# Redistributing the modulation matrix's chunks over the stages of a two-block kernel

## The reference

```python
cs = jax.nn.silu(c)
for layer in range(DEPTH):
    mod = jnp.matmul(cs, ada_w[layer]) + ada_b[layer]
    sh_m, sc_m, g_m, sh_f, sc_f, g_f = [m[:, None, :] for m in jnp.split(mod, 6, axis=-1)]
    h = modulate(x, norm_mix_g[layer], sh_m, sc_m)
    y = (even_mixer, odd_mixer)[layer](h, ...)
    x = x + (g_m * y).astype(x.dtype)
    h = modulate(x, norm_ffn_g[layer], sh_f, sc_f)
    x = x + (g_f * conv_glu_ffn(h, ...)).astype(x.dtype)
```

## Time and profile before

| | |
|---|---|
| time, median of 3 runs | 2181.15 us (2172.75 to 2181.36) |
| the profiled execution's own time | 2180.79 us |
| its span, first to last instruction | 2179.0 us |
| mean granted clock of TensorE | 0.976 |
| TensorE busy | 95% |
| VectorE, ScalarE, GpSimd busy | 48%, 36%, 36% |
| read from HBM | 199.1 MB, 92 GB/s over the span |

### The profile page before, as it was taken

One profiled execution on the slowest core, in us unless ns is written; L12 is line 12 of the kernel. 1 busy time (PEld: TensorE's weight loads), 2 busy tenths in 40 slices (PEclk: granted clock), 3 DMA queues, 4 the chain that ended last, 5 costly groups with the idle time before them and its releaser, 6 DMA issues.

```text
span 2179.0 us, 22946 instructions
## 1 busy us (share of the span) xinstructions
PE 2062.0 (95%) x9468; PEld 1572.6 (72%) x9468; DVE 1053.4 (48%) x1507; ACT 780.9 (36%) x1186; POOL 782.9 (36%) x333
## 2 busy tenths in 40 slices
PE   7998999889999999997999998999999999999998
PEld 5765667588856679884778877886975577788886
DVE  6356575654466666914275546635601343211233
ACT  3332564423355332135342312324355433322231
POOL 3313363134354344221234334433423233434432
PEclk9999999999989999998999999999999999999999
DMA  5226202155510244110125344423311022233321
GB/s 177 90 89 161 78 1 68 60 175 173 174 59 21 97 135 136 59 59 20 58 77 160 111 134 137 149 90 97 97 59 39 20 97 78 78 97 98 108 62 62
DMA packets 202728, 203.54 MB, mean 93 GB/s; under 512 B 11871, under 2 KB 199523, under 8 KB 202624
## 3 DMA queue, kind: packets, MB, share of 16 engines
q1 hardware_dynamic: 200953, 200.90, 28.9%
q0 software_dynamic: 656, 1.01, 0.3%
q10 hardware_dynamic: 1015, 0.16, 0.0%
HBM read 199.10 MB, written 2.10 MB: 92 GB/s over the span
## 4 chain that ended last, share of the span: by engine, by line
PE 69%; DVE 14%; ACT 7%; POOL 6%; DMA 2%; issue 2%; SPq 0%; DVEq 0%; ACTq 0%; POOLq 0%
PE bank L505 40%; PE bank L950 14%; POOL wl L2024 6%; ACT wh L1164 3%; PE bank L687 2%; DVE var L1578 2%; DVE acc L1546 2%; PE bank L711 1%; PE bank L807 1%; PE bank L736 1%; DVE conv L1917 1%; DVE conv L1919 1%; PE bank L1009 1%; DVE conv L1915 1%; PE bank L1030 1%
## 5 line engine op out<-in xcount | busy, mean ns | idle before, releaser
L2024 POOL TENSOR_TENSOR wl<-ring,wh 128x2048 fp32r<-128x2048 f32 (+3 forms) x150 | 643.0, 4288 | 1099.3 <-ACT wh L1164 1099.3
L1164 ACT ACTIVATE wh<-ring 128x2048 fp32r<-128x2048 f32 (+3 forms) x150 | 265.1, 1768 | 286.1 <-PE bank L950 95.3
L1546 DVE SCALAR_TENSOR_TENSOR acc<-ring,cs,acc 128x256 f32<-128x256 f32 x336 | 287.5, 856 | 12.0
L505 PE MATMUL bank<-xfh,wh 128*128 128x512 f32 x704 | 278.2, 395 | 15.6 <-POOL wl L2024 12.7
L505 PE MATMUL bank<-xfh,wl 128*128 128x512 f32 x704 | 275.0, 391 | 0.0
L505 PE MATMUL bank<-xfl,wh 128*128 128x512 f32 x704 | 274.9, 391 | 0.0
L505 PEld LDWEIGHTS bank<-xfh,wh 128*128 128x128 f32 x704 | 132.6, 188 | 51.1 <-POOL wl L2024 17.4
L505 PEld LDWEIGHTS bank<-xfh,wl 128*128 128x128 f32 x704 | 132.6, 188 | 28.2
L1894 DVE SCALAR_TENSOR_TENSOR x<-bank,mod,x 128x512 f32<-128x512 f32 x48 | 34.7, 750 | 243.0 <-PE bank L950 243.0
L505 PEld LDWEIGHTS bank<-xfl,wh 128*128 128x128 f32 x704 | 132.8, 189 | 26.6
L950 PE MATMUL bank<-hsph,wh 128*128 128x512 f32 x352 | 138.8, 394 | 4.7 <-POOL wl L2024 4.7
(11 more groups left out here) (386 smaller groups left out, 4277.4 us busy)
## 6 DMA issues: line engine op xcount, KB each, us to landing
ring<-in_ada_w SPq DMA_DIRECT2D x48, 1024.0 KB, 5.3
ring<-in_ffn_w_in SPq DMA_DIRECT2D x44, 1024.0 KB, 5.2
ring<-in_w_in_b SPq DMA_DIRECT2D x14, 1024.0 KB, 5.3
ring<-in_even_w_in SPq DMA_DIRECT2D x14, 1024.0 KB, 5.2
ring<-in_ffn_w_out SPq DMA_DIRECT2D x16, 768.0 KB, 4.9
ring<-in_odd_w_in SPq DMA_DIRECT2D x12, 1024.0 KB, 5.3
ring<-in_ffn_w_out SPq DMA_DIRECT2D x16, 640.0 KB, 4.4
ring<-in_w_out SPq DMA_DIRECT2D x8, 1024.0 KB, 5.1
```

Source lines behind the costliest of these rows:

```text
L505: mm = eng.matmul(o, l_, r_, start=(first and i == 0), stop=(last and i == 2))
L1164: eng.activation(wh[:, m % SPLIT, 0:w], ring[:, n % RING, 0:w], ACT.Copy).then_inc(wh_ready, 1)
L1546: ins = eng.scalar_tensor_tensor(out=s, in0=w[:, k, :], scalar=cs[:, k:k + 1], in1=s, op0=ALU.mult, op1=ALU.add)
L2024: eng.tensor_tensor(wl[:, m % SPLIT, 0:w], ring[:, n % RING, 0:w], wh[:, m % SPLIT, 0:w].bitcast(F32), ALU.subtract).then_inc(wl_ready, 1)
```

## The change

The ada chunks stand elsewhere in the plan, by explicit lists: none in the first gate projection; none behind the first chunk of layer b's value projection and one behind each of the 13 others; none behind the even mixer's first chunk (5 there); in the first FFN's third and fifth pair of part one a second one, between a and g; seven in the odd mixer, behind the last three qk chunks and the four v chunks. VectorE's calls follow: `ada_steps(6)` before the rotations goes, 15 becomes 13, 6 becomes 5, two steps instead of one in the two FFN pairs, and in the odd mixer one step behind the convolutions of tiles 3, 5 and 7 and four behind the last. The modulation is taken in four parts of 24 columns, when 19, 24, 41 and 48 sums are made (`ADA_UNTIL`): before the even mixer, behind the even mixer's ada steps, in the FFN's second part, and in the odd mixer before `gcol`. `shift` on ScalarE waits for its own part. TensorE has an `ada_sums(0)` more behind the even mixer's ia chunks and one behind v, and `lag=1` in qk and v of the odd mixer.

```diff
-ADA_FIRST = 26
+ADA_UNTIL = (19, 24, 41, 48)
+ADA_TWICE = {0: (2, 4), 12: ()}
...
-    def add(chunks, per=0):
+    def add(chunks, behind=()):
         for n, c in enumerate(chunks):
             plan.append(c)
-            for _ in range((n + 1) * per // len(chunks) - n * per // len(chunks)):
+            for _ in range(behind[n] if n < len(behind) else 0):
                 plan.append(ada.pop(0))
...
-    add(k8("in_a.gate", w, 928, 1952), 6)
+    add(k8("in_a.gate", w, 928, 1952))
...
-    add(k8("out_a", a["w_out"][0], 0, D), 3)
+    add(k8("out_a", a["w_out"][0], 0, D), (0, 1, 1, 1))
...
-        + k8("in_b.k", w, MAIN, 2 * MAIN), 15)
-    add(k8("out_b", a["w_out"][1], 0, D), 3)
+        + k8("in_b.k", w, MAIN, 2 * MAIN), (0,) + 13 * (1,))
+    add(k8("out_b", a["w_out"][1], 0, D), (0, 1, 1, 1))
...
+    for name, lo, behind in (("qa", 0, (0, 1)), ("fa", 512, (1, 1)), ("ia", 1024, (1, 1)), ("ga", 1536, ()), ("qb", 2048, ()),
...
+            pairs = zip(k8(f"ffn{l}.a", w, lo * P, hi * P), k8(f"ffn{l}.g", w, FFN + lo * P, FFN + hi * P))
+            for n, (x, g) in enumerate(pairs):
+                add([x, g], (int(n in ADA_TWICE[lo]), 1) if l == 0 else ())
...
     add(k8("odd.gates", w, 3008, 3088) + k8("odd.qk", w, 0, 1024) + k8("odd.v", w, 1024, 2048)
-        + k8("odd.og", w, 2048, 3072))
+        + k8("odd.og", w, 2048, 3072), (0, 0) + 7 * (1,))
+    assert not ada
...
-                    if j >= ADA_FIRST:
-                        pe.wait_ge(mod_ready, 2)
+                    taken = sum(j >= n for n in ADA_UNTIL)
+                    if taken:
+                        pe.wait_ge(mod_ready, taken)
...
             project("even.ia", 2, "act", "x_even", xe, tok=True, lag=1)
+            ada_sums(0)
...
-            project("odd.qk", 4, "act", "x_odd", xo, fill=3)
-            project("odd.v", 4, "act", "x_odd", xo, tok=True)
+            project("odd.qk", 4, "act", "x_odd", xo, lag=1, fill=3)
+            project("odd.v", 4, "act", "x_odd", xo, tok=True, lag=1)
+            ada_sums(0)
...
-            act.wait_ge(mod_ready, 2)
...
             def shift(l, part, tmp, dst):
+
+                act.wait_ge(mod_ready, 1 + 2 * l + part // 3)
...
-            ada_steps(6)
             for h in range(HEADS):
...
-            ada_steps(15)
+            ada_steps(13)
...
+            def modulation(l, half):
+
+                n = 2 * l + half
+                cols = slice(24 * n, 24 * n + 24)
+                dve.wait_ge(ada_summed, ADA_UNTIL[n])
+                chain.link(eng.tensor_tensor(mod[:, cols], mod_bank[:, cols], vecs[:, P + 24 * n:P + 24 * n + 24], ALU.add))
+                tile, row, _ = VEC_ROWS[("norm_mix_g_2", "norm_ffn_g_2")[half]]
+                g = vecs[:, tile * P + row + 8 * l:tile * P + row + 8 * l + 8]
+                eng.scalar_tensor_tensor(out=gmod[:, n, :], in0=mod[:, 24 * n + 8:24 * n + 16], scalar=1.0, in1=g,
+                                         op0=ALU.add, op1=ALU.mult).then_inc(mod_ready, 1)
+                dve.wait_ge(mod_ready, n + 1)
+
+            modulation(0, 0)
...
-            ada_steps(6)
+            ada_steps(5)
+            modulation(0, 1)
...
                             if l == 0:
-                                ada_steps(1)
+                                ada_steps(2 if (t0 - lo) // 2 in ADA_TWICE[lo] else 1)
...
                     if l == 0 and part == 1:
-                        modulation(1)
+                        modulation(1, 0)
...
                         ins.then_inc(qk_conv, 1)
+                if t in (3, 5, 7):
+                    ada_steps(1)
+            ada_steps(4)
+            modulation(1, 1)
             b = take(dve, ("gcol",), "dve")
```

More of the change, by code:

```diff
@@ L144, in weight_plan @@
     add(k8("in_b.v", w, 2 * MAIN, 3 * MAIN) + k8("in_b.qm", w, 2316, 2572) + k8("in_b.gate", w, 2572, 3596) + k8("in_b.q", w, 0, MAIN)
-        + k8("in_b.k", w, MAIN, 2 * MAIN), 15)
-    add(k8("out_b", a["w_out"][1], 0, D), 3)
+        + k8("in_b.k", w, MAIN, 2 * MAIN), (0,) + 13 * (1,))
+    add(k8("out_b", a["w_out"][1], 0, D), (0, 1, 1, 1))
     w = a["even_w_in_2"][0]
-    for name, lo, per in (("qa", 0, 2), ("fa", 512, 2), ("ia", 1024, 2), ("ga", 1536, 0), ("qb", 2048, 0),
-                          ("kb", 2560, 0), ("vb", 3072, 0)):
-        add(k8("even." + name, w, lo, lo + 512), per)
+    for name, lo, behind in (("qa", 0, (0, 1)), ("fa", 512, (1, 1)), ("ia", 1024, (1, 1)), ("ga", 1536, ()), ("qb", 2048, ()),
+                          ("kb", 2560, ()), ("vb", 3072, ())):
+        add(k8("even." + name, w, lo, lo + 512), behind)
     add(k8("even_out", a["even_w_out_2"][0], 0, D))
@@ L157, in ffn @@
         for lo, hi in FFN_PARTS:
-            for x, g in zip(k8(f"ffn{l}.a", w, lo * P, hi * P), k8(f"ffn{l}.g", w, FFN + lo * P, FFN + hi * P)):
-                add([x, g], min(len(ada), 1))
+            pairs = zip(k8(f"ffn{l}.a", w, lo * P, hi * P), k8(f"ffn{l}.g", w, FFN + lo * P, FFN + hi * P))
+            for n, (x, g) in enumerate(pairs):
+                add([x, g], (int(n in ADA_TWICE[lo]), 1) if l == 0 else ())
             half = (hi - lo) // 2
@@ L162, in ffn @@
                 add([(f"ffn{l}.out", v[:, t:t + half, c:c + CHUNK], half, CHUNK) for t in (lo, lo + half)],
-                    int(l == 0 and lo == 0))
+                    (0, int(l == 0 and lo == 0)))
     ffn(0)
-    assert not ada
     w = a["odd_w_in_2"][0]
     add(k8("odd.gates", w, 3008, 3088) + k8("odd.qk", w, 0, 1024) + k8("odd.v", w, 1024, 2048)
-        + k8("odd.og", w, 2048, 3072))
+        + k8("odd.og", w, 2048, 3072), (0, 0) + 7 * (1,))
+    assert not ada
     add(k8("odd_out", a["odd_w_out_2"][0], 0, D))
@@ L1467, in _ @@
             ffn(0)
-            act.wait_ge(mod_ready, 4)
             shift(1, 0, tmp_o, xo)
@@ L1755, in _ @@
             eng.tensor_scalar(fr[4], fr[3], -1.0, None, ALU.mult).then_inc(frows_ready, 1)
-            ada_steps(15)
+            ada_steps(13)
             attention(1)
             out_first(1)
[L1759 to L1764, removed]
-                for n, (part, name) in enumerate([(1, "norm_mix_g_2"), (4, "norm_ffn_g_2")]):
-                    tile, row, _ = VEC_ROWS[name]
-                    g = vecs[:, tile * P + row + 8 * l:tile * P + row + 8 * l + 8]
-                    c = 48 * l + 8 * part
-                    eng.scalar_tensor_tensor(out=gmod[:, 2 * l + n, :], in0=mod[:, c:c + 8], scalar=1.0, in1=g,
-                                             op0=ALU.add, op1=ALU.mult).then_inc(mod_ready, 1)
-                dve.wait_ge(mod_ready, 2 * (l + 1))
-            modulation(0)
+            def modulation(l, half):
[9 more added lines that the diff above has]
+            modulation(0, 0)
             def modulated(j, l, part, tmp, dst):
```

## The result

The changed kernel takes 2215.11 us (median of 4 runs, 2208.23 to 2217.77), the kernel before, run beside it, 2179.18 us (median of 4). The ratio is 1.0165, with a 95% interval of 1.0132 to 1.0198: slower by 36 us. The profiled execution took 2213.69 us, its span is 2212.0 us and its mean granted clock 0.972 (before 0.976).

What follows compares the result with a forecast made beforehand. TensorE, busy 2062 of 2179 us, was taken as the bound, so only its gaps count. Terms -10.2-8.0-4+2.6+24.6+36.7 = +41.7 on 2180.8 gave 2222 us, range 2203 to 2245.

Steps and rivals of the forecast that it cites:

- term 3: Second attention's start: the last ada step is over before VectorE's first row maxima; -4 us, bounds -7.3 and -1.2.
- term 6: Odd mixer: loads of qk3, v0 and v1 wait for late ada steps, TensorE idles three times; +36.7 us, bounds +28 and +42.
- First gate stage: Six ada chunks out of the first gate projection, so the weights are not late; -10.2 us, bounds -12 and -8.
- Layer b's start: Second block's projection: the third value chunk's load no longer waits for an ada step; -8.0 us, bounds -9 and -6.
- Even mixer: Gap before its third chunk goes, but the variance waits for the 19th sum; +2.6 us, bounds -2 and +5.
- FFN's doubles: First FFN, third and fifth pair: the next a load waits for a late ada step; +24.6 us, bounds +20.6 and +30.
- the loads are in time: Rival for the FFN and odd mixer: no new stalls, only the gains are left; 2161 us, chance 0.08.
- Half of it: Rival: one stall in the odd mixer (12 us) and the FFN's doubles at half price (12); 2185 us, chance 0.04.
- The clock stays low between the stalls: Rival: TensorE runs whole chunks behind the FFN stalls and in v1 at 1.2 GHz; 2249 us, chance 0.06.
- The starts pay nothing: Rival: the waits removed at the stages' starts were covered by others; 2244 us, chance 0.04.
- ScalarE's waits for `in_odd_w_in`: Sign in the odd mixer: ScalarE's high part waits three times for that ring load, some 10 us each.

Runs made afterwards that it cites:

- experiment 5: Against the changed kernel: four ada chunks in the gate stage, no doubled FFN pairs, five in the odd mixer, modulation at 22, 28, 43, 48 sums; 2162.16 us.
- experiment 4: Changed kernel without the doubled FFN pairs; those two ada chunks stand behind the first gate stage's second and third chunk; 2191.4 us.
- Experiment 7: Changed kernel with one ada chunk behind layer b's first value chunk again and none behind the projection's last chunk; 2216.42 us.
- experiment 3: Changed kernel with the ada chunk behind layer b's last but one projection chunk moved behind the last, which then has two; 2220.15 us.
- experiment 2: Changed kernel with the first part of the modulation taken at 18 sums instead of 19; 2203.0 us.
- 6: Changed kernel with both ada chunks of the FFN's third and fifth pair behind g instead of one on either side; 2193.93 us.
- 1: Changed kernel with the odd mixer's first three ada steps behind the convolutions of tiles 1, 3, 5 instead of 3, 5, 7; 2189.65 us.
- 8: Changed kernel with one ada chunk behind layer b's first value chunk and two behind the projection's last chunk; 2231.81 us.

## Why the prediction was right

The forecast was 2222 us with a range of 2203 to 2245. The runs gave 2215.11, with the sum of the ledger at +33 us for the predicted +41.7. That the total comes so near is in part luck: term 3 missed by 8 us on one side and term 6 by 4.6 on the other. By its own steps:

1. *First gate stage*: -10.2 predicted, -11.0 in the ledger. Right; experiment 5 puts one ada chunk behind the first gate chunk and the detour returns, experiment 4 puts two elsewhere and it doesn't.
2. *Layer b's start*: -8.0 predicted, -7.9 in the ledger. Experiment 7 alone gives 5.8 us for it in its trace, and no difference of the medians that stands out of the spread. So the term fitted the two traces, but neither the gap nor the clock part (2.8 us of the 8) is the same each time.
3. *Second attention's start*: the term of the sum that was mis-sized. Predicted -4 with bounds of -7.3 and -1.2, measured -12.0, outside the bounds. The late start itself is worth some 3 us, 5.0 with the half clock near the attention's end (experiment 3), about the value taken. The bounds left the half clock behind the start out, though the text called it open: 17.1 us at 0.50 can cost up to 8.5 us, and it cost 8. A stretch that is named as open belongs into the bounds with its full price.
4. *Even mixer*: +2.6 predicted, +2.0 measured; its loss of 8.8 came out at 8.1 (experiment 2).
5. *FFN's doubles*: +24.6 predicted, +22.9 measured, gaps of 8.24 and 7.91 us for the 8.5. Experiments 4 and 6 take 23 and 19 us of it away, 6 without removing a step.
6. *Odd mixer*: +36.7 predicted, +41.3 measured. Up to the transposes `gcol` the chain was right: they stand at 1628.49 with a lag of -8.3 at the stage's start, 37.2 us later than the 1599.57 of the earlier trace rows. The prediction had qk3, v0 and v1 ready at 1554.5, 1576.3 and 1598.0, less the lag 1546.2, 1568.0 and 1589.7; TensorE starts them at 1546.08, 1568.56 and 1589.70. The gaps are shorter than the 11.1, 10 and 10 (26.3 us in sum for 31) because the chunks ahead of the second and third run slowly, 13.42 and 14.48 us, and that hides under the chain, as the prediction said. Only v1's 14.18 us count, a loss of 2.7 for the 2.0. The other 4 us lie behind the transposes, where the prediction had nothing and the first heads run for 6.8 us at half clock:

```profile
1568.60:1583.00 14.40, 14.40 (x98) 14.40 (x99) 12.48 (x24) 0.00 (x0) 0.00 (x0) 0.79 0.28 87
...
1636.20:1643.00 6.80, 6.80 (x17) 5.07 (x16) 1.62 (x3) 4.86 (x6) 4.95 (x5) 0.50 0.22 68
```

From the transposes to the out projection's first low part the kernel before has 3.4 us of half clock and the changed kernel 13.7. Experiments 6, 4 and 1, with 7.7, 7.2 and 10.4 us of it, are 1.0, 0.8 and 2.4 us longer there than the kernel before, the changed kernel 4.1. So the term left out is clock behind the transposes. The 2.0 us for a gap was about right: single gaps cost 1.6 (experiment 7) to 2.8 us, each of the three in a row 2.2 to 3.0.

Among the rivals, *the loads are in time* would need the detour to be absent, and it stands in the trace five times. *Half of it* had one stall in the odd mixer; there are three. *The clock stays low between the stalls* has the right place (v1 and behind) but not the size: the chunks behind the gaps run at 0.79 to 0.82 in the odd mixer and at 0.86 in the FFN on average, not at 0.50. *The starts pay nothing* is refuted by the earlier trace rows having no counterpart and by experiment 5, and for layer b by experiment 7's trace. The sign was shown too: the two changes that lose are the doubled pairs and the odd mixer, and each, undone in its order alone (6 and 1), gives back 21 us (19 in the ledger) and 25 us.

What the forecast of a row got wrong: ScalarE's waits for `in_odd_w_in` are 15.4, 19.6 and 16.3 us, not some 10. A wait of ScalarE is longer than the gap of TensorE that it causes, because TensorE still had a chunk to work off while ScalarE already waited.

## What to carry to other kernels

In a ring of three slots that one queue fills in order, an item with a slow consumer delays not itself but the load three places behind it: find for each such item which load hangs on its end, and put it where that load is wanted late (the same two steps cost 2 us behind g and 11.5 around it). When items are moved away from a gap, price the places they go to by the same chain (end of the step, load, high part, low part) and look first for idle time of their engine, such as VectorE's before the even mixer's diagonal. Read a threshold on a shared counter from both sides: 19 of 19 sums made the consumer wait for the last one, 42 of 43 made the producer wait for the consumer.

## What the runs showed of the hardware

**The same stage at several clocks.** The same second attention took 99.8, 100.6, 104.75 or 111.8 us by what stood ahead of it, and the 12 us of both causes together are more than the sum of each. Why is open. Where the two traces of the kernel before agree on it within 0.05 us, the clock in the first attention does not: the changed kernel and its variants 1, 2, 3, 6, 7 and 8 are the same program up to there, and the stretch from the last split before to the first split behind the attention took 101.56 us with no half clock in it, 102.8 to 102.9 with 3.4 us of it, and 105.28 with 10.2 us. The Trainium skill, "TensorE: Matmul & The Clock Gate", section "Part 1", says that the number of slow matmuls at a kernel's start differs from run to run. These traces show such a difference 250 us behind the start as well, with up to 3.7 us.

**The spread of the runs goes with the clock.** Nine executions of the kernel before on one chip range from 2169.92 us at a mean clock of 0.983 to 2183.27 at 0.975, and the times between go nearly in that order. A difference under some 5 us between two single traces of this kernel should be looked up in the low-clock stretches before it is put down to an edit.

**VectorE behind GpSimd.** Many operations of VectorE that start beside a low-part split last until the split ends. VectorE's timeline in the odd mixer of the changed kernel, then GpSimd's:

```profile
1541.97 4.33 DVE L1966 TENSOR_SCALAR qkc<-qk_raw,vecs 128x512 f32<-128x512 f32 x1 [7.76 <-ACT qk_raw L1175]
...
1541.53 4.50 POOL L2031 TENSOR_TENSOR wl<-ring,wh 128x2048 fp32r<-128x2048 f32 x1 [23.06 <-ACT wh L1169]
```

4.33 us for 0.54 undisturbed. All 28 operations of ada steps that start so in this trace (0.6 us or more ahead of the split's end) end 0.15 to 0.29 us behind the split. Those that read a result bank don't wait: 15 of `prod<-bank,gel` beside a split took 0.68 to 0.69 us, as elsewhere. The Trainium skill, "SBUF — State Buffer", section "Who interferes with whom", describes, for certain kinds of operation, a port pair that the two engines share, held for a whole instruction by the one that starts first, while the other waits in full. The trace agrees for this operation: it ends 0.27 us behind the split.
